# Even and odd prompt queries, sample states on four column strips, and a new order of the small products

## What is computed

```python
GROUPS = ((128, 1), (512, 4), (2048, 16))      # window, dilation; 2 heads of 64 each
# prompt: query q of a group sees key k if k <= q, (q - k) % dilation == 0, q - k <= window;
# softmax over all three groups together, then the sum of probabilities times values
# sample: one query a sequence against its cache (8 sequences)
# recurrence, 4 heads, keys and values of 64:
S = f * S + k^T v                              # sample: one step for each of the 8 sequences
o = q S                                        # then a norm by head, silu gate
```

## Time and profile before

| | us |
|---|---|
| median of 3 timed runs | 821.97 (819.72 to 823.34) |
| profiled execution, its own time | 821.23 |
| its span, first to last instruction | 819.4 |
| TensorE busy | 808.2 (99%) |
| VectorE, ScalarE, GpSimd busy | 568.5, 439.7, 267.1 |
| mean granted TensorE clock | 0.995 |

### The profile page before, as it was taken

How to read it: one execution, slowest core, us unless ns; L and a number is a source line. 1 busy time by engine, 2 the same in 40 slices (tenths; PEclk the granted TensorE clock), 3 DMA queues, 4 the chain that set the end, 5 groups by cost and what they waited for, 6 DMA issues and landing times.

```text
span 819.4 us, 17912 instructions
## 1 busy us (share of the span) xinstructions
PE 808.2 (99%) x6902; PEld 795.0 (97%) x6902; DVE 568.5 (69%) x776; ACT 439.7 (54%) x627; POOL 267.1 (33%) x240
## 2 busy tenths in 40 slices
PE   8999999999999999999999999999999999999996
PEld 8998999999999999999999999999999999999996
DVE  7979697677877665544577777866787676645552
ACT  6663385645566664444354635674555666644442
POOL 3597192055700000122139626702564000001220
PEclk9999999999999999999999999999999999999998
DMA  9896879668567778767559977997665777786751
GB/s 312 238 333 249 305 213 332 216 230 296 179 196 236 244 256 294 261 241 247 189 171 258 327 253 240 278 266 244 234 223 180 253 252 231 255 282 235 254 205 53
DMA packets 171034, 199.95 MB, mean 244 GB/s; under 512 B 19680, under 2 KB 168624, under 8 KB 169648
## 3 DMA queue, kind: packets, MB, share of 16 engines
q1 hardware_dynamic: 169040, 196.48, 73.0%
q10 hardware_dynamic: 1936, 2.66, 0.9%
HBM read 191.21 MB, written 51.90 MB: 297 GB/s over the span
## 4 chain that ended last, share of the span: by engine, by line
PE 91%; DVE 4%; POOL 3%; ACT 1%; issue 0%; ACTq 0%; DVEq 0%; POOLq 0%
PE main L672 27%; PE main L673 27%; PE main L674 27%; PE small L672 1%; PE small L674 1%; PE small L673 1%; PE small L688 1%; DVE w_lo L1251 1%; POOL k_lv L1713 1%; POOL cum_f L1722 1%; PE small L717 1%; POOL suf_f L1719 1%; PE small L729 1%; DVE h_lo L1267 1%; POOL v_cache L1703 0%; PE small L830 0%
## 5 line engine op out<-in xcount | busy, mean ns | idle before, releaser
L1000 ACT ACTIVATE w_hi<-raw 128x1024 fp32r<-128x1024 f32 (+1 forms) x256 | 266.2, 1042 | 243.8 <-PE main L674 165.6
L1251 DVE TENSOR_TENSOR w_lo<-raw,w_hi 128x1024 fp32r<-128x1024 f32 (+1 forms) x256 | 339.0, 1325 | 68.2 <-ACT w_hi L1000 66.3
L672 PE MATMUL main<-h_hi,w_hi 128*128 128x264 f32 x1248 | 359.5, 288 | 0.1
L673 PE MATMUL main<-h_lo,w_hi 128*128 128x264 f32 x1248 | 354.9, 284 | 0.0
L674 PE MATMUL main<-h_hi,w_lo 128*128 128x264 f32 x1248 | 354.6, 284 | 0.0
L672 PEld LDWEIGHTS main<-h_hi,w_hi 128*128 128x128 f32 x1248 | 236.0, 189 | 3.4 <-issue 1.1
L673 PEld LDWEIGHTS main<-h_lo,w_hi 128*128 128x128 f32 x1248 | 236.2, 189 | 0.2
L674 PEld LDWEIGHTS main<-h_hi,w_lo 128*128 128x128 f32 x1248 | 235.0, 188 | 0.0
L672 PE MATMUL main<-a_hi,w_hi 128*128 128x264 f32 x512 | 145.4, 284 | 0.0
L674 PE MATMUL main<-a_hi,w_lo 128*128 128x264 f32 x512 | 145.2, 284 | 0.0
L673 PE MATMUL main<-a_lo,w_hi 128*128 128x264 f32 x512 | 145.2, 284 | 0.0
(11 more groups left out here) (241 smaller groups left out, 1042.4 us busy)
## 6 DMA issues: line engine op xcount, KB each, us to landing
raw<-in_w_in SPq DMA_DIRECT2D x48, 1024.0 KB, 6.5
raw<-in_w_up SPq DMA_DIRECT2D x32, 1024.0 KB, 5.4
raw<-in_w_down SPq DMA_DIRECT2D x32, 1024.0 KB, 5.4
out_kvs<-in_cache SPq DMA_DIRECT2D x48, 512.0 KB
out_kvs<-in_cache SPq DMA_DIRECT2D x32, 496.0 KB
raw<-in_w_o SPq DMA_DIRECT2D x8, 1024.0 KB, 5.5
raw<-in_w_br SPq DMA_DIRECT2D x8, 768.0 KB, 4.9
gates<-q_scratch SPq DMA_DIRECT2D x4, 768.0 KB, 7.4
```

What stands on the lines that cost most here:

```text
L672: pe.matmul(out[:, 0:TOK], wh, rh, start=start and k == 0, stop=False)
L673: pe.matmul(out[:, 0:TOK], wh, rl, start=False, stop=False)
L1000: act.activation(w_hi[:, slot(l, u), 0:k, :], raw_of(u, k), ACT.Copy).then_inc(w_hi_ready, 1)
L1251: dve.tensor_tensor(w_lo[:, slot(l, u), 0:k, :], raw_of(u, k), w_hi[:, slot(l, u), 0:k, :].bitcast(F32), ALU.subtract).then_inc(w_lo_ready, 1)
```

## The change

1. `TURNS` and the levels: level 6 alone at place 14, levels 7 and 8 at place 16. The mask of level 7 stands in VectorE's turn 16, the copy of level 8 in ScalarE's turn 17. Place 17 waits as before.
2. Rotation: sine on four tiles in turn 14, cosine on four and sine on two in turn 15, cosine on two in turn 16, without a wait of VectorE for each; the sum in turn 17 as before, the outer product behind it in turn 18.
3. Prompt queries are taken as even and odd ones (`prompt_part`). In the groups with dilation 4 and 16 an even query sees only even keys, so that each part needs 256 + 128 + 128 keys: 4 blocks of 128 for each head and part, 16 in all. Queries and keys are read with a step of two, and so are keys and values of these groups where they are transposed (kv_tm is kept by parity, and stored with a step of two rows). The masks are 1024 columns for 1152.
4. Sample recurrence: GpSimd builds `q_wide` (zeros, then the queries of both heads in eight of 32 columns). At place 21 four products of 32 output rows and 256 columns run on four column strips (line 762 of the new kernel); VectorE keeps each sequence's own part and sums (turn 21, lines 1607 and 1611); place 23 turns the rows into columns with two products (line 772). The 32 products of place 24 are gone. GpSimd adds the outer product after `q_heads`.
5. Small products: places 15, 24 and 28 are gone, place 16 is new: 15 places. The norm products of place 28 stand at 30, with the sample scores of place 32; all transposes of probabilities at 32; the keys' and values' transposes at 23 (groups 0 and 1) and 30 (group 2). The turns of ScalarE and VectorE that read them move along: exponentials in turns 23 and 25 for 26, scaling in 27 and 28 for 28, sample sums one turn earlier, reciprocals in 32 and 33 for 30 and 31.

Stores of `kv_s` and `kv_tm` move one weight pair later.

```diff
+LEVELS_AT = ((10, (2, 3)), (12, (4, 5)), (14, (6,)), (16, (7, 8)))
...
+        def prompt_part(tile, g, part):
+            first, step = (part * P, 1) if g == 0 else (part, 2)
+            return tile[:, first:first + (P - 1) * step + 1:step]
...
+            def scores(l, part):
+                banks = [use_bank(pe, l, f"scores {h} {part}") for h in range(2)]
+                for g in range(NG):
+                    at, n = ((0, PROMPT), (PROMPT, P), (PROMPT + P, P))[g]
+                    for h in range(2):
+                        rows = slice(h * HD, (h + 1) * HD)
+                        queries = prompt_part(z[rows, CT_Q + g, :], 1, part)
+                        keys = z[rows, CT_K + g, 0:PROMPT] if g == 0 else prompt_part(z[rows, CT_K + g, :], g, part)
+                        mm = pe.matmul(banks[h][:, at:at + n], queries, keys, start=True, stop=True)
...
+            def sample_states(l):
+                pe.wait_ge(state_s_ready, l + 1)
+                pe.wait_ge(q_wide_ready, l + 1)
+                bank = use_bank(pe, l, "sample states")
+                for part in range(4):
+                    hp, bs = part // 2, slice(part % 2 * 4, part % 2 * 4 + 4)
+                    mm = pe.matmul(bank[part * 32:part * 32 + 32, 0:4 * HD], q_wide[:, hp, part % 2, :], state_s[:, bs, hp, :],
+                                   start=True, stop=True)
...
             def attend(l):
+                for part in range(2):
+                    blocks = [(0, 0), (0, 1), (1, part), (2, part)]
+                    for i, (g, keys) in enumerate(blocks):
...
-                if u in (10, 12, 14):
-                    level(l, u - 8)
-                    level(l, u - 7)
-                if u == 15:
-                    level(l, 8)
+                for at, numbers in LEVELS_AT:
+                    if u == at:
+                        for i in numbers:
+                            level(l, i)
...
-                    if u == 15:
-                        dve.wait_ge(halves_swapped, l * 8 + 8)
-                        step(dve.tensor_tensor(swapped_qk, swapped_qk, sin.unsqueeze(1).to_broadcast([P, 6, TOK]), ALU.mult))
-                    if u == 16:
-                        step(dve.tensor_tensor(z[:, CT_Q:CT_V, :], z[:, CT_Q:CT_V, :],
-                                               cos.unsqueeze(1).to_broadcast([P, 6, TOK]), ALU.mult))
+                    for turn, tile, table, t0, t1 in ((14, swapped_qk, sin, 0, 4), (15, z[:, CT_Q:CT_V, :], cos, 0, 4),
+                                                      (15, swapped_qk, sin, 4, 6), (16, z[:, CT_Q:CT_V, :], cos, 4, 6)):
+                        if u == turn:
+                            dve.wait_ge(halves_swapped, l * 8 + (4 if t0 == 0 else 8))
+                            dve.tensor_tensor(tile[:, t0:t1, :], tile[:, t0:t1, :],
+                                              table.unsqueeze(1).to_broadcast([P, t1 - t0, TOK]), ALU.mult)\
+                               .then_inc(rope_parts, 1)
...
-                    if u in (10, 12, 14):
-                        mask_level(u - 8)
-                        mask_level(u - 7)
+                    for turn, numbers in LEVELS_AT:
+                        if u == turn:
+                            for i in numbers:
+                                if i < 8:
+                                    mask_level(i)
...
+                step(pool.memset(sample_parts[:, 0:P], 0.0))
+                for h in range(2):
+                    step(pool.tensor_copy(q_wide[rows, :, :, h * 4:h * 4 + 4], z[rows, CT_CQ:CT_CQ + 2, PROMPT:TOK].rearrange(
+                        "p a (j b) -> p a j b", j=2)))
```

More of the change, by code:

```diff
@@ L85 @@
     + ["sample q T", "scores 0 0", "scores 1 0"]
[3 rows of a table removed]
-    + ["head norm 0", "head norm 1"]
-    + [f"probs T {i}" for i in range(5)]
-    + ["sample scores T", "attend", "sample probs T", "sample attend", "sample attend T"]
[3 rows of a table added]
+    + [f"probs T {i}" for i in range(4)]
+    + ["attend", "sample probs T", "sample attend", "sample attend T"]
     + [f"branch {m} {j}" for m in range(KT) for j in range(3)]
@@ new lines, in sample_rows, with sample_kvs @@
+            def sample_rows(l):
+                pe.wait_ge(state_rows_ready, l + 1)
+                bank = use_bank(pe, l, "sample recurrence")
+                for h in range(2):
+                    c = K_SEL + h * 2 * SAMPLES
+                    mm = pe.matmul(bank[h * HD:(h + 1) * HD, 0:2 * SAMPLES], state_rows,
+                                   consts[:, c:c + 2 * SAMPLES], start=True, stop=True)
+                done(mm, "sample recurrence")
+            def sample_kvs(first, end):
+                return [z[:, (CT_K, CT_V)[i % 2] + i // 2, PROMPT:TOK] for i in range(first, end)]
@@ L734, in attend, with keys_values @@
+            def keys_values(l, g):
+                transposes(l, f"kv T {g}", [((part * 2 + kv) * P, prompt_part(z[:, (CT_K, CT_V)[kv] + g, :], g, part))
+                                            for part in range(2) for kv in range(2)])
             def attend(l):
[L735 removed]
+                pe.wait_ge(probs_t_ready, l * 4 + 4)
                 bank = use_bank(pe, l, "attend")
[L737 to L741 removed]
@@ L843, in between @@
                              f"head norm {hp}")
[L844 to L850 removed]
+                if u == 30:
                     pe.wait_ge(s_scored, l + 1)
@@ L861, in between @@
                     done(mm, name)
+                    keys_values(l, 2)
+                if u == 32:
+                    pe.wait_ge(weighed, l * 4 + 4)
+                    for i in range(4):
+                        transposes(l, f"probs T {i}", [(b * P, probs[:, i // 2, i % 2, b * P:b * P + P])
+                                                       for b in range(ROW_BLOCKS)])
                 if u == 35:
@@ L1826, in constants @@
             c[b * 2 + h, K_HSEL + h * HD:K_HSEL + (h + 1) * HD] = 1.0
+    for part in range(4):
+        for h in range(2):
+            for b in range(4):
+                row = part * 32 + h * 4 + b
+                c[row, K_OWN + b] = 1.0
+                c[row, K_SEL + h * 2 * SAMPLES + part * 4 + b] = 1.0
     return c
```

227 lines of the change are left out of this document (106 added, 121 removed), and 6 rows, old and new, of the table TURNS.

## The result

| | before | changed |
|---|---|---|
| median, us | 819.69 (6 runs, 819.61 to 823.34) | 816.11 (6 runs, 816.03 to 816.58) |
| ratio, 95% interval | | 0.993 (0.991 to 0.995) |
| profiled execution, own time / span | 821.23 / 819.4 | 816.09 / 814.3 |
| mean granted clock in it | 0.995 | 0.998 |

The account below looks back on a forecast made before the run. TensorE's own work, busy 808.2 of 819.4 us, plus its few waits bounds the kernel. 821.23 - 3.8 (work) - 1.9 (old waits) + 4.8 (new wait) - 1.5 + 1.5 (clock) = 820.3, stated as 820.5; range 814.5 to 825.

Parts of the forecast that it names:

- The new wait: Place 17: TensorE waits for level 7's mask from VectorE, 2.2 us in the first layer, 2.6 in the second, +4.8.
- cosine waits 0.6, the two splits 0.8 and the last split 1.9 behind the scaling: Second layer, before level 7's mask: VectorE operations held up by GpSimd, so the mask ends at 472.5.
- rival 1: Place 17: the mask is in time; 814.0, or 816 with a rest of 1 us in each layer; chance 0.31.
- the forecast's lower edge: Place 17: forecast held for one wait of 1.5 to 3.5 us in each layer, 817.5 to 823.5 in time.
- A new fall of the clock: Behind place 17: idleness of 2.6 us brings one fall of TensorE's clock in two passes, +1.5 (between 0 and 3).
- The old fall: Behind line 830's one-column products, second layer: without them the half clock's cost goes, -1.5 us.
- Work: TensorE's products removed and added: -1.9 us a layer, -3.8 for two.
- two ends more, 0.2: State products and the two 16-column products stand among other shapes, adding about two shape changes, 0.2 us a layer.
- places 15 and 28 bring nothing by themselves: Removing these places gains nothing: level 8 moves to place 16, place 28's norm products and transposes cost the same elsewhere.
- Waits that go: First layer: waits at place 14 for GpSimd's keys (-0.3) and place 19 for VectorE's recurrence copy (-1.6) vanish, -1.9.
- Step of two: Scores and transposes: weight loads from every second element cost nothing extra, 0; the bound was 3 us a layer.
- Strips overlap: Place 21: four state products of 256 columns on four strips overlap, 0.15 us each, 0.6 together.

## Why the prediction missed

**The new wait, forecast +4.8, measured +3.0: this is the step that failed.** Place, releaser and both layers were right; the size was not (2.6 and 2.2 forecast, 1.42 and 1.40 measured). The words were "cosine waits 0.6, the two splits 0.8 and the last split 1.9 behind the scaling", 3.3 in all. Measured in the second layer were 0.5 for the sine, 0.55 for one split, 1.4 for the cosine and nothing for the last split, 2.45 in all. The mechanism stands, as the run without scaling shows. What went wrong was which operation meets the scaling. By the prediction's own terms the last split would begin 9.3 us after place 14 does (7.9 of free durations and 1.4 of holds), with the scaling beside it until 11.2. In the trace place 14 begins at 456.10 and the scaling ends at 466.01, 9.9 later. It came in one VectorE operation earlier, right behind the split at 463.00. An evacuation, which GpSimd doesn't hold up, covered 0.35 of it, the short cosine waited 1.4 for the rest, and the last split found the way free. That is 0.85 of the 1.2 that the wait was shorter; the rest is small pieces. Why the prediction's queue had the scaling later isn't on record and stays open. It wasn't the copies into `q_wide`. They stood in it with 0.4, which is right where nothing is in their way, as in the run with the levels back:

```profile
461.39 0.19 POOL L1776 COPY gates<-z 64x16 f32<-64x16 f32 x1 [0.17 <-POOL gates L1772]
461.74 0.20 POOL L1776 COPY gates<-z 64x16 f32<-64x16 f32 x1 [0.16 <-POOL gates L1776]
```

In the changed kernel they took longer, 0.99 and 0.46 (461.51 to 463.13): the first ended with VectorE's cosine (462.46), the second with its sine (463.07). That moved the scaling later, not earlier. For the first layer the prediction gave its 2.2 without terms, so only this can be said: the scaling, which it took for the main hold, comes behind the mask there, and GpSimd's other work made the holds. The rivals had named the weak point ("a shift of GpSimd's scaling by 1 us into VectorE's masks would take most of the wait away") and put 0.31 on it; the wait of 1.4 lies between rival 1's rest of 1 and the forecast's lower edge of 1.5.

**A new fall of the clock, forecast +1.5, measured 0.** It followed from the size above: behind 1.4 us no fall came, behind 3.1 and more it did. For waits of 2.2 and 2.6, as forecast, the runs leave it open: with waits of 2.0 and 2.5 in the second layer one run of eleven and three of twelve lay a step higher. So the term was wrong by the same error, and one fall in the two passes may have been too much even for its own waits.

**The old fall, -1.5: right in sum, too simple in reasoning.** The two runs with products at place 24 show that the one-column products bring such a fall. That nothing else comes in its place was not asked. In the profiled execution of the kernel before a split was next by 0.37 us. The full 1.5 came in the changed kernel, where what stands around that split was moved too. That was luck: the prediction gave no reason for it.

**Work, forecast -3.8, measured -4.5.** In each layer place 24 gave 2.18 for 2.16 and place 35 0.22 for 0.2. Places 19, 21 and 23 became 0.77 longer, but 0.42 of it are four transposes that stood at place 28. Without them it is 0.35, where the forecast had 0.6 + 0.16 + 0.2 - 0.3 = 0.66. Start to start, the strips took 0.57 for 0.6, the two products that turn rows into columns 0.23 for 0.16, the scores 0.36 less for 0.3. The "two ends more, 0.2" hardly came (0.07), and the transposes of 8x128 took 0.17 less. Places 28, 30 and 32 became 0.63 shorter, 0.37 of it by the four transposes; the rest is near the 0.2 forecast. There the ends of place 28 go, 0.2, but the norm products take 0.19 more at place 30, so that "places 15 and 28 bring nothing by themselves" was about right.

**Waits that go, forecast -1.9, measured -2.3.** Both went, by 1.7 and 0.6. The outer product alone does it at place 19, as its own run shows.

**Step of two, forecast 0, measured 0.4 at most**, though each such load of a transpose takes 64 ns longer. **Strips overlap:** right, four in 0.57. Place 21 found its states. From place 14 of the first layer to the end of the second no product waits for a split or for weights, so the moved stores and the fuller turns cost nothing that shows.

Errors: +1.8 for the wait, +1.5 for the clock, +0.7 for work, +0.4 for waits. All had the same sign. They add up to 4.4; the sum of 820.3 missed the profiled 816.1 by 4.2, since the pieces that were measured overshoot the spans by 0.2.

## What to carry to other kernels

Where an operation that TensorE waits for stands at the end of a VectorE turn behind operations that another engine can hold up, move it ahead of them; here the move of one mask brought 3.0 more, beside the 6.0 of the whole change on the same chips. When the queues of two engines that hold each other up are laid beside each other, what matters is which operation meets which: one place earlier, and GpSimd's scaling of 1.94 us cost 1.4 and not 1.9, and of another operation. Both queues are held up, the copies of 0.2 us on GpSimd too (0.99 and 0.46). So give such a wait as a range as wide as the longest of these operations, and let every term that hangs on it (the clock) range with it. Before counting a removed slowdown as a gain, ask which buffer would have been late had it not been there.

## What was not expected of the hardware

- Two microseconds of one-column products (64x64 weights) brought TensorE's granted clock to half (0.50) for about 3 us, worth 1.5 us, in some passes and not in others; wide products of the same length in the same place did not in the profile. Idle stretches of 3.1, 3.4, 3.6 and 4.5 us did it in the profiles, 1.4, 2.0 and 2.5 us did not; by the runs' times and mean clocks 3.1 us does it in most passes only.
- One small VectorE operation (256 columns) took 0.41 us in one layer and 1.52 in the other, beside other work of GpSimd. It goes both ways: a copy of 16 columns on GpSimd took 0.99 beside VectorE's cosine and 0.19 where no such operation stood beside it.
- Weight loads from every second element: 205 ns for 141 (transposes), 193 for 187 (scores), nearly all of it hidden.
